# Small float32 matmuls issued in two halves of the array's columns

## The reference

```
xf * lax.rsqrt(jnp.mean(xf * xf, axis=-1, keepdims=True) + RMS_EPS)          # every norm: a sum of squares
sc = jnp.einsum('bqgrd,bngd->bgrqn', qc, kc).astype(jnp.float32) * scale     # compressed scores
o_w = jnp.einsum('bgrqk,bkgd->bqgrd', p_w.astype(vwc.dtype), vwc)            # attention values
x * lax.rsqrt(jnp.sum(x * x, axis=-1, keepdims=True) + EPS)                  # l2 norm of keys and queries
```

## Time and profile before

| | us |
|---|---|
| median of 3 runs | 1586.87 |
| lowest and highest run | 1586.11, 1588.28 |
| profiled execution, whole | 1586.05 |
| its span in the trace | 1584.2 |
| PE matmul busy | 1531.3 (97%) |
| PE weight loads busy | 1437.0 (91%) |
| DVE busy | 1028.0 (65%) |

### The profile page before, as it was taken

How to read it: one execution, slowest core, us unless ns; L and a number is a source line. 1 busy time by engine, 2 the same in 40 slices (tenths; PEclk the granted TensorE clock), 3 DMA queues, 4 the chain that set the end, 5 groups by cost and what they waited for, 6 DMA issues and landing times.

```text
span 1584.2 us, 28579 instructions
## 1 busy us (share of the span) xinstructions
PE 1531.3 (97%) x11138; PEld 1437.0 (91%) x11138; DVE 1028.0 (65%) x1792; ACT 836.2 (53%) x1638; POOL 351.3 (22%) x403
## 2 busy tenths in 40 slices
PE   7799999999988989999999999999999999999998
PEld 6389999999988989999999999999999888888886
DVE  4255567555576875476999976777775555555554
ACT  4166455444456543445444457777775554545454
POOL 1133431000155463321465540001112000000000
PEclk9899999999998999999999999999999999999999
DMA  9732455555433442356445554444444656666664
GB/s 216 224 107 81 133 184 169 178 183 186 160 108 113 146 139 77 106 168 195 147 159 174 174 184 151 146 136 145 137 144 162 196 191 196 189 197 194 192 196 137
DMA packets 76771, 254.20 MB, mean 160 GB/s; under 512 B 11375, under 2 KB 15293, under 8 KB 76509
## 3 DMA queue, kind: packets, MB, share of 16 engines
q1 hardware_dynamic: 76397, 251.71, 49.9%
q0 software_dynamic: 240, 0.66, 0.2%
HBM read 250.23 MB, written 1.84 MB: 159 GB/s over the span
## 4 chain that ended last, share of the span: by engine, by line
PE 80%; DVE 12%; DMA 2%; ACT 2%; POOL 2%; issue 1%; SPq 1%; POOLq 0%; DVEq 0%; ACTq 0%
PE bank L675 78%; DVE wl L1661 4%; DVE big L1661 2%; POOL big L2341 2%; DMA big<-in_w1k 1%; ACT big L1236 1%; DVE big L1664 1%; ACT wh L1236 1%; DVE big L2187 1%; DVE big L2198 1%; DVE big L2194 1%; DVE big L2183 1%; DVE big L2204 1%; DVE big L2191 1%; PE bank L984 1%
## 5 line engine op out<-in xcount | busy, mean ns | idle before, releaser
L1661 DVE TENSOR_TENSOR wl<-raw,wh 128x1024 fp32r<-128x1024 f32 (+4 forms) x459 | 531.5, 1159 | 399.5 <-ACT wh L1236 398.9
L1236 ACT ACTIVATE wh<-raw 128x1024 fp32r<-128x1024 f32 (+1 forms) x459 | 482.2, 1053 | 351.3 <-PE bank L675 333.1
L675 PE MATMUL bank<-gw,wh 128*128 128x256 f32 x3504 | 651.3, 287 | 2.4 <-DVE big L1664 2.4
L675 PEld LDWEIGHTS bank<-gw,wh 128*128 128x128 f32 x3504 | 547.4, 193 | 3.0 <-DVE big L1664 2.8
L675 PE MATMUL bank<-gw,wl 128*128 128x256 f32 x1752 | 497.7, 284 | 6.4 <-POOL wl L2341 5.0
L675 PEld LDWEIGHTS bank<-gw,wl 128*128 128x128 f32 x1752 | 336.8, 192 | 8.0 <-issue 6.3
L675 PE MATMUL bank<-xw,wh 128*128 128x256 f32 x1696 | 321.9, 290 | 9.9 <-ACT wh L1236 7.5
L675 PE MATMUL bank<-wh,xw 128*128 128x512 f32 x1056 | 326.9, 391 | 0.0
L675 PEld LDWEIGHTS bank<-xw,wh 128*128 128x128 f32 x1696 | 267.9, 194 | 16.8 <-ACT wh L1236 7.8
L1236 ACT ACTIVATE big<-bank 128x256 f32<-128x256 f32 (+23 forms) x326 | 118.5, 373 | 260.6 <-PE bank L675 222.7
L2341 POOL TENSOR_TENSOR wl<-raw,wh 128x384 fp32r<-128x384 f32 (+3 forms) x131 | 175.6, 1346 | 336.9 <-ACT wh L1236 336.9
(11 more groups left out here) (136 smaller groups left out, 1107.7 us busy)
## 6 DMA issues: line engine op xcount, KB each, us to landing
raw<-in_wst SPq DMA_DIRECT2D x455, 512.0 KB, 3.6
big<-toeplitz SPq DMA_DIRECT2D x8, 256.0 KB, 14.2
big<-in_w1k SPq DMA_DIRECT2D x4, 512.0 KB, 18.1
big<-in_w1v SPq DMA_DIRECT2D x4, 512.0 KB, 19.4
big<-in_xT SPq DMA_DIRECT2D x4, 256.0 KB, 5.0
raw<-in_wst SPq DMA_DIRECT2D x4, 256.0 KB, 4.7
big<-in_keys SPq DMA_DIRECT2D x1, 1024.0 KB, 5.5
out<-big SPq DMA_DIRECT2D x4, 256.0 KB, 2.4
```

Of the source, the lines that this page charges most:

```text
L675: return e.matmul(o, a, b, start=first, stop=last, skip_group_check=True)
L1236: return e.activation(o, x, f, **kw)
L1661: return e.tensor_tensor(o, a, b, f)
```

## The change

A helper `columns` is added, which issues a matmul as two: the first on weight columns 0 to 63, with the result in partitions 0 to 63 of the bank, the second on columns 64 to 127, with the result in partitions 64 to 127. The moving operand is the same for both. Five calls use it in place of `mm`. The semaphore is still raised by the last matmul, now the second half.

```
+                def columns(o, a, b, first=True, last=True):
+
+                    for r in (slice(0, 64), slice(64, 128)):
+                        z = mm(o[r, :], a[:, r], b, first, last)
+                    return z
...
-                        mm(o, ACC[:, half(tile)], ones[:, 0:1], True, False)
+                        columns(o, ACC[:, half(tile)], ones[:, 0:1], True, False)
...
-                            z = mm(o, ring(n, c)[:, half(tile)], ones[:, 0:1], False, c == 7)
+                            z = columns(o, ring(n, c)[:, half(tile)], ones[:, 0:1], False, c == 7)
...
-                            z = mm(banks[6 + tile][:, 32 * c:32 * c + 32], QN[:, c, half(tile)], KCT)
+                            z = columns(banks[6 + tile][:, 32 * c:32 * c + 32], QN[:, c, half(tile)], KCT)
...
-                            z = mm(banks[6 + run % 2][:, 64 * h:64 * h + 64], PTS[s % 4][:, half(m * nb + j)],
-                                   V[:, j, v:v + 64], j == 0, j == nb - 1)
+                            z = columns(banks[6 + run % 2][:, 64 * h:64 * h + 64], PTS[s % 4][:, half(m * nb + j)],
+                                        V[:, j, v:v + 64], j == 0, j == nb - 1)
...
-                                z = mm(b[:, 4 * tile + h:4 * tile + h + 1], SQ4[:, h, half(tile)], ones[:, 0:1])
+                                z = columns(b[:, 4 * tile + h:4 * tile + h + 1], SQ4[:, h, half(tile)], ones[:, 0:1])
```

## The result

| | before | after |
|---|---|---|
| median, us | 1586.06 (6 runs, 1585.36 to 1588.28) | 1580.49 (6 runs, 1578.07 to 1582.46) |
| ratio | | 0.9962, 95% interval 0.9949 to 0.9975 |
| profiled execution, and its span | 1586.05, 1584.2 | 1580.16, 1578.4 |

The change is 5.6 us faster (the interval of the ratio makes that 4.0 to 8.1); the forecast was 1579.4, between 1575 and 1583. The page of after shows the same picture as the earlier trace rows: first the busy time of each engine, then the chain that ended last.

A forecast was written before the change was run, and what follows sets the result against it. PE was taken to bound the kernel, busy 124.98 of 125.00 us from 50 to 175 us. Gains of 7.5 us from 1586.05 gave 1578.5, or 1579.4 at the median's level; forecast between 1575 and 1583, range 1575 to 1587.5.

The forecast's parts named there:

- What bounds the kernel: PE sets the pace, busy 124.98 of 125.00 us from 50 to 175 us; time saved there reaches the end.
- What a half costs: In split groups, two 64-column halves load at once, a pair every 0.056 us against 0.112 for a whole record.
- The change of shape: At each group's edges, 0.21 us going in, 0.054 + 0.09 coming out, and a bare wide load of 0.11.
- The sum: Gains over all counted groups, from attention values to key and query norms, add up to 7.5 us.
- turns: Sums of squares at 235 and 427 us, with drains falling into waits, gain 0.8 us.
- the group at half clock: Key and query norms at 498 us, at 1.2 GHz: everything doubles, gain 1.1 us.
- What is late next: In the attention stage nothing becomes late, since DVE and ACT have half their time free.
- Not counted, 555 us: Group at 555 us gives nothing because POOL's substitution is the chain there; without that cover, 0.55 us.
- halves taking turns: Rival: in split groups the two halves load one after the other, 7.2 us lost, 1594.1; 14 in 100.
- issue running dry: Rival: in groups of 16, pairs beyond 16 arrive every 0.056 us, gain only 3.9, 1583.0; 7 in 100.
- nothing tiled: Rival: 64-column matmuls follow each other at 0.056 us without drain, no change, 1586.9; 6 in 100.
- no overlap of load and stream: Rival: each half of a values record takes 0.11 us, 15.6 on top of 1594, about 1610; 2 in 100.

The follow-up runs named there:

- e3: The changed kernel with all first halves issued before all second halves within a step; 1585.45 us, ratio 0.9996.
- e8: The changed kernel with only every second matmul of attention values split, the others whole; 1589.92 us in one run.
- e5: The changed kernel with the group of sums at 555 us issued whole again; 1578.49 us in one run.
- e2: The changed kernel with attention values and compressed scores whole again, only sums of squares halved; 1583.43 us, ratio 0.9985.
- e4: The changed kernel with each split matmul in four parts of 32 weight columns instead of two of 64; 1575.12 us, ratio 0.9922.
- e10: The changed kernel itself, unaltered, measured again on another chip; 1578.11 us, ratio 0.9954.

## Why the prediction was right

- *What bounds the kernel*: right for the stages. But not every group on PE's path gave its gain to the end: the norms at 447 and 743 us, counted with 0.1 each, gave none, and 0.6 of the attention stage and up to 0.9 at the diag chain are lost.
- *What a half costs*: 0.056 us for a pair was predicted from row tiles and 30-column loads; 0.058 it is. That two column halves load together was an analogy from row tiles; the traces of after and e3 show it. (The 61 ns that the range allows for an issue in order have no row behind them.)
- *The change of shape*: 0.21 going in, exactly. Coming out 0.054 + 0.09 was predicted, 0.152 measured with 64 moving columns and 0.127 with one. The bare load behind is there. e8 gives nearly the same price, 0.30 us for a way in and out. That a change of tiling mode drains TensorE, as the Trainium skill has it (TensorEngine Tiling (Array Packing), section Key Properties), agrees with all of it: a round trip costs 0.34 us with 64 moving columns and 0.29 with one, by the groups of 8 and 16, and within a group of one shape nothing.
- *The sum*: the terms of the table add up to 3.6 (values), 0.34, 0.4 (norms), 0.7 (turns), 1.1 and 1.6: 7.8 us, for 7.5 predicted. Mis-sized: values, predicted 3.9 and measured 3.6, and the group at half clock, 1.1 and 1.6. There I had doubled everything, the way in and out too. The loads nearly doubled (0.213 us for each whole record and not 0.112, 0.107 for a pair of halves and not 0.058), but the way in cost nothing: PE stands still for 0.41 us ahead of this group in before as in after ("0.41 <-issue", and the row below), and the way out took 0.175 us and not 0.25.
```profile
493.85 1.81 PEld L675 LDWEIGHTS bank<-ones,big 128*64 128x64 f32 x32 [0.41 <-issue]
495.68 0.50 PEld L675 LDWEIGHTS bank<-gw,wh 128*128 128x128 f32 x2
```

- *What is late next: "in the attention stage nothing"*: this step was wrong. I read DVE's share of the stage (56.57 of 125 us) and not the one chain of DVE that PE waits for at each turning of the features, which ended just as PE came for it. It cost 0.5 us.
- *Not counted, 555 us*: right (e5). But the cover reaches further than that group: the chain of diag begins at 533 us, and PE's gain ahead of it passes only as far as the chain's own start came earlier (0.3 to 0.5 us less in after, e2, e4 and e10). The chain's own length does the rest: 0.6 are lost in after and 0.9 in e10, and in e5, with its short chain, 1.0 is won.
- *That the number came so close is in part luck.* e10, whose half-clock windows from 50 us on match those of before, ends 7.86 - 1.27 = 6.6 us earlier than before once the first weights have arrived. The way there from 7.8 is: 0.6 less for the attention stage, 0.3 for the two norms, 0.3 that the groups at 498 and 519 us give less together than each by itself, 0.9 for the diag chain; and 1.0 more for the wait at 528 us that is gone, which the prediction didn't have. That makes 6.7. In after's profile the window at 582 us takes another 1.6, and 5.0 are left.
- *Rivals*: halves taking turns is refuted by the pairs of after; issue running dry by e4; nothing tiled by the idle stretches at the edges of each group; no overlap of load and stream by the 0.058 us of a pair whose two parts alone would be 0.11. The rule of the Trainium skill (TensorE: Matmul & The Clock Gate, section Part 3, The mechanism), that a load passes beside a matmul only where the row group differs, doesn't hold in this trace: both column halves use all 128 rows, and their loads and matmuls lie over each other. (The same section also lets a load pass that goes to the background weight buffer; no row here tells whether that is what happens.)

What stays open: why the half-clock windows fall where they do; whether halves gain nearer to 5.6 or to 8.3 us, which the intervals don't part; and how the halved sums end the wait at 528 us.

## What to carry to other kernels

A small matmul that is bound by its 128-column weight load (here 0.112 us for each record with 64 or fewer moving columns) can be halved or quartered by columns, with the parts next to each other in program order, where at least six to eight records stand together; lone ones lose 0.20 us. Quarters are the better choice where one column moves, and bring little where 64 do. And before a gain of PE is counted, read for each product that PE comes to fetch how long it has been ready: an engine that is idle for half of the stage can be late in the one place.

## What the runs showed of the hardware

- Pairs of load and matmul for four column parts start 0.0084 us apart on average (64 in 0.54 us, e4); two halves start 0.006 to 0.007 us apart (after), and within one half loads of 64 columns follow each other every 0.058 us (e3).
- In e3's groups of values one half starts at most three pairs ahead of its turn; everything behind these waits in line, though its part is free.
- At half clock (granted 0.50, 1.2 GHz) a whole record of sums takes 0.213 us and not 0.112 and a pair of halves 0.107 and not 0.058, but the way out of the halves 0.175 us and not twice 0.127.
- Going into column halves and out again costs 0.34 us with 64 moving columns and 0.29 with one, in groups of 8 and of 16 records alike.
